# ScalarE instead of VectorE copies attention's turned probabilities, and the work ahead of the second block's output projection is put in another order

## What is computed

```python
for l in range(2):                                   # first block
    x = x + 0.5 * swiglu_ffn(rms_norm(x), ...)
    uv, c_q, c_kv, k_rope, z, xbc, dt, gates = split(rms_norm(x) @ w_in)
    merged = (g0 * (gmlp(uv) @ w_branch0)
              + g1 * (mla(c_q, c_kv, k_rope) @ w_branch1)     # causal attention, 8 heads
              + g2 * (ssd(z, xbc, dt) @ w_branch2))
    x = x + merged @ w_out
    x = x + 0.5 * swiglu_ffn(rms_norm(x), ...)
# second block
o = delta_rule(...); o = o * rsqrt(mean(o*o) + eps) * gain * silu(z)      # 512 columns
y = gelu(s5(u));     y = y * sigmoid(y @ w_glu + b_glu)                   # 512 columns
x = x + concat(o, y) @ w_out
x = x + cross_attention(rms_norm(x), mem)
return rms_norm(x + swiglu(rms_norm(x)))
```

## Time and profile before

| | us |
|---|---|
| Median of 3 runs (lowest, highest) | 1829.95 (1828.91, 1839.23) |
| The profiled execution | 1829.92 |
| Its span on the core, first to last instruction | 1828.1 |
| TensorE busy in the span | 1789.1 (98%) |
| VectorE busy | 1046.3 (57%) |
| ScalarE busy | 818.6 (45%) |
| GpSimd busy | 77.6 (4%) |

### The profile page before, as it was taken

How to read it: one execution, slowest core, us unless ns; L and a number is a source line. 1 busy time by engine, 2 the same in 40 slices (tenths; PEclk the granted TensorE clock), 3 DMA queues, 4 the chain that set the end, 5 groups by cost and what they waited for, 6 DMA issues and landing times.

```text
span 1828.1 us, 27099 instructions
## 1 busy us (share of the span) xinstructions
PE 1789.1 (98%) x11448; PEld 1584.1 (87%) x11448; DVE 1046.3 (57%) x1226; ACT 818.6 (45%) x885; POOL 77.6 (4%) x145
## 2 busy tenths in 40 slices
PE   8999999999999999999999999999999999999998
PEld 8998797877999899987978779998887976889996
DVE  4555356887655455553669876455666534545553
ACT  4554345552654445543555526544123123535542
POOL 0000000000000000000000001000561100000000
PEclk9999999999999999999999999999999999999999
DMA  7537255444655645372555446855254223436371
GB/s 253 184 125 282 81 165 160 156 148 138 207 180 192 213 151 184 120 286 81 165 164 159 141 138 208 186 196 207 92 162 79 72 90 115 139 122 213 126 276 58
DMA packets 194332, 293.15 MB, mean 160 GB/s; under 512 B 9298, under 2 KB 128884, under 8 KB 194244
## 3 DMA queue, kind: packets, MB, share of 16 engines
q1 hardware_dynamic: 191988, 287.72, 46.6%
q0 software_dynamic: 1936, 4.14, 2.1%
q10 hardware_dynamic: 320, 0.01, 0.0%
HBM read 289.49 MB, written 2.36 MB: 160 GB/s over the span
## 4 chain that ended last, share of the span: by engine, by line
PE 90%; DVE 4%; ACT 3%; DMA 2%; issue 1%; ACTq 0%; DVEq 0%; SPq 0%
PE acc L225 22%; PE acc L226 22%; PE acc L227 22%; PE acc L271 3%; PE acc L194 2%; PE acc L206 2%; PE acc L3030 2%; PE acc L462 1%; DMA ring<-in_ffn_w_in 1%; PE acc L2725 1%; PE acc L253 1%; PE acc L1304 1%; ACT big L1432 1%; ACT part_hi L216 1%; PE turn L1409 1%
## 5 line engine op out<-in xcount | busy, mean ns | idle before, releaser
L430 DVE TENSOR_TENSOR w_lo<-ring,w_hi 128x2048 fp32r<-128x2048 f32 x160 | 361.9, 2290 | 211.4 <-ACT w_hi L426 211.3
L225 PE MATMUL acc<-xT_hi,w_hi 128*128 128x256 f32 x1680 | 476.0, 283 | 1.2 <-DVE w_lo L430 0.8
L227 PE MATMUL acc<-xT_hi,w_lo 128*128 128x256 f32 x1680 | 475.4, 283 | 0.0
L226 PE MATMUL acc<-xT_lo,w_hi 128*128 128x256 f32 x1680 | 475.4, 283 | 0.0
L426 ACT ACTIVATE w_hi<-ring 128x2048 fp32r<-128x2048 f32 x160 | 301.3, 1912 | 150.1 <-PE acc L227 99.6
L225 PEld LDWEIGHTS acc<-xT_hi,w_hi 128*128 128x128 f32 x1680 | 322.5, 192 | 1.7 <-DVE w_lo L430 1.0
L226 PEld LDWEIGHTS acc<-xT_lo,w_hi 128*128 128x128 f32 x1680 | 322.5, 192 | 0.0
L227 PEld LDWEIGHTS acc<-xT_hi,w_lo 128*128 128x128 f32 x1680 | 322.5, 192 | 0.0
L225 PE MATMUL acc<-w_hi,hT_hi 128*128 128x512 f32 x440 | 172.3, 392 | 0.0
L227 PE MATMUL acc<-w_hi,hT_lo 128*128 128x512 f32 x440 | 171.3, 389 | 0.0
L226 PE MATMUL acc<-w_lo,hT_hi 128*128 128x512 f32 x440 | 171.3, 389 | 0.0
(11 more groups left out here) (550 smaller groups left out, 2978.7 us busy)
## 6 DMA issues: line engine op xcount, KB each, us to landing
ring<-in_ffn_w_in SPq DMA_DIRECT2D x88, 1024.0 KB, 6.1
ring<-in_w_in SPq DMA_DIRECT2D x52, 1024.0 KB, 5.0
ring<-in_ffn_w_out SPq DMA_DIRECT2D x44, 1024.0 KB, 6.4
ring<-in_w_branch SPq DMA_DIRECT2D x12, 1024.0 KB, 5.1
ring<-in_w_out SPq DMA_DIRECT2D x12, 1024.0 KB, 4.9
ring<-in_w_gate SPq DMA_DIRECT2D x11, 1024.0 KB, 5.2
ring<-in_w_up SPq DMA_DIRECT2D x11, 1024.0 KB, 6.8
ring<-in_w_down SPq DMA_DIRECT2D x11, 1024.0 KB, 6.0
```

Source lines behind the costliest of these rows:

```text
L225: pe.matmul(o, a_hi, wh, start=start, stop=False)
L226: pe.matmul(o, a_hi, wl, start=False, stop=False)
L227: return pe.matmul(o, a_lo, wh, start=False, stop=stop)
L430: vec.tensor_tensor(w_part(w_lo, r), raw_part(c0, r), w_part(w_hi, r).bitcast(F32), ALU.subtract).then_inc(f.lo, 1)
```

## The change

Two edits. First, in both layers the six copies of the turned probabilities become ScalarE's: `qs_vec6` turns into `qs_act4`, and stands in ScalarE's order between the high part of chunk 7 and that of chunk 8. TensorE's waits for these copies are moved from VectorE's counter to ScalarE's (the copies count 20 to 25 there), and VectorE's counter ends at 48 instead of 54. Second, in the second block `rc_vec` is cut in three (`rc_vec`, `rc_out_vec`, `rc_turned_vec`), `glu_vec` moves ahead of the norm of o, the y half is split before the o half, and on both engines the rest or high part of chunk 1 is put between them. TensorE's products of chunk 0 now wait for both halves' `late_x_lo`, since that of o comes second.

```diff
@@ qs_pt_pe, qs_vec6, qs_pv_pe @@
                 for r, (m, kb, hf) in enumerate(TURNS):
                     pe.wait_ge(qs.vec, 44 + 2 * m)
                     if r >= 4:
-                        pe.wait_ge(qs.vec, 47 + r - 4)
+                        pe.wait_ge(qs.act, 20 + r - 4)
...
-            def qs_vec6(vec):
+            def qs_act4(act):
                 for r, (m, kb, hf) in enumerate(TURNS):
-                    vec.wait_ge(qs.pe, 17 + r)
+                    act.wait_ge(qs.pe, 17 + r)
                     dst = PT1[:, kb, 4 * hf:4 * hf + 4, :] if m else PT0[:, 4 * hf:4 * hf + 4, :]
-                    vec.tensor_copy(dst, turn[r % 4][:, :].rearrange("p (h n) -> p h n", h=4)).then_inc(qs.vec, 1)
+                    act.activation(dst, turn[r % 4][:, :].rearrange("p (h n) -> p h n", h=4), ACT.Copy).then_inc(qs.act, 1)
             def qs_pv_pe(pe):
-                pe.wait_ge(qs.vec, 52)
+                pe.wait_ge(qs.act, 25)
...
-            BRANCH_IN = {0: (gm.vec, 7), 1: (qs.vec, 54), 2: (sd.vec, 31)}
+            BRANCH_IN = {0: (gm.vec, 7), 1: (qs.vec, 48), 2: (sd.vec, 31)}
@@ mixer_act @@
-                tail_part_act(act, 6, 7, 8)
+                tail_part_act(act, 6, 7)
+                qs_act4(act)
+                tail_part_act(act, 8)
                 branch_in_act(act, 2)
@@ mixer_vec @@
                 tail_part_vec(vec, 7)
                 branch_gate_vec(vec, 0, 1)
-                qs_vec6(vec)
                 tail_part_vec(vec, 8)
@@ second block @@
-        def out2_x_act(act):
-            for i, ready in enumerate(((rc.vec, RC_DONE), (gl.vec, GLU_DONE))):
-                act.wait_ge(*ready)
-                act.activation(late_x_hi[:, 4 * i:4 * i + 4, :], xT[:, 4 * i:4 * i + 4, :], ACT.Copy).then_inc(late.act, 1)
...
+        def out2_x_act(act, i):
+            act.wait_ge(*((rc.vec, RC_DONE), (gl.vec, GLU_DONE))[i])
+            act.activation(late_x_hi[:, 4 * i:4 * i + 4, :], xT[:, 4 * i:4 * i + 4, :], ACT.Copy).then_inc(late.act, 1)
+
+        def out2_x_vec(vec, i):
+            ks = slice(4 * i, 4 * i + 4)
+            vec.wait_ge(late.act, LATE_X["out2"] + 2 - i)
+            vec.tensor_tensor(late_x_lo[:, ks, :], xT[:, ks, :], late_x_hi[:, ks, :].bitcast(F32), ALU.subtract).then_inc(late.vec, 1)
@@ rc_vec @@
                     ins.then_inc(rc.vec, 1)
+
+        def rc_out_vec(vec):
             for m in range(MT):
                 vec.wait_ge(rc.act, 5 + m)
...
+        def rc_turned_vec(vec):
             for m in range(MT):
                 vec.wait_ge(rc.pe, 13 + m)
@@ second_pe @@
-            late_group_pe(pe, G_WO2, 0, (1, 2))
+            late_group_pe(pe, G_WO2, 0, (2, 2))
@@ second_act @@
-            late_act(act, 0, 1)
-            out2_x_act(act)
+            late_act(act, 0)
+            out2_x_act(act, 1)
+            late_act(act, 1)
+            out2_x_act(act, 0)
             late_act(act, 2)
@@ second_vec @@
             rc_vec(vec)
+            glu_vec(vec)
+            rc_out_vec(vec)
             late_vec(vec, 0)
-            glu_vec(vec)
+            out2_x_vec(vec, 1)
+            rc_turned_vec(vec)
             late_vec(vec, 1)
-            out2_x_vec(vec)
+            out2_x_vec(vec, 0)
             late_vec(vec, 2, 3, 4, 5)
```

## The result

| | before | changed |
|---|---|---|
| Median, us (lowest to highest, 10 runs each) | 1836.92 (1828.91 to 1843.73) | 1820.79 (1816.13 to 1828.28) |
| Ratio, 95% interval | | 0.9936 [0.9918, 0.9955] |
| The profiled execution / its span, us | 1829.92 / 1828.1 | 1821.73 / 1820.0 |

The account below looks back on a forecast made before the run. TensorE was taken to bound the kernel, 90% of the span, losing time at three stalls and the slow clock behind them. 3.80 + 3.75 + 4.99 = 12.54 us off 1829.92 gave 1817.4 us, range 1814 to 1823.

Parts of the forecast that it names:

- Which stalls, and what they cost: TensorE's waits: 4.2 us in two for attention's copies, 3.2 us in one for `late_x_lo` at the projection; all would go.
- Attention's way: TensorE from first transpose to the values' products: 12.26 and 12.21 us, to save 3.80 in layer 0, 3.75 in layer 1.
- The projection's 4.99: Second block's output projection: products end 4.99 us earlier, 3.16 of them idle time and 1.83 slow clock.
- ScalarE keeps up: At attention ScalarE is free, copies take 0.62 us each, nothing waits; they would start to cost at 0.9 us.
- Rival 3: At attention ScalarE's copies are slow, 2 us each, so the first edit gives nothing: 1824.9 us; 3%.
- The second block's order: VectorE's new order ends the last `late_x_lo` at 1529.02, 0.58 us before TensorE can use it.
- rival 2: A new small stall at the projection, 0.5 us and at worst 1.83 us of clock: about 1820 us; 10%.
- Clock: 4.8 us at the three places: Behind the three stalls the clock stays up once they are gone, 4.8 us of the predicted gain.
- one or two falls put into the range: Behind the first edit clock falls may appear or vanish; one or two, about 1.6 us each, widen the range.
- So each stall costs twice: At the three stalls TensorE loses the wait and then a slow clock: 0.43 us per product instead of 0.23.
- Rival 4: In layer 1's second feed-forward part, chunks come later, 16.8 us lost: 1834 us; 3%.
- A run of this kernel can be told from no change from about 1%: For the whole kernel, 18.3 us needed to tell a change: 1811.6 or 1848.2; within 95%, faster 3%, slower 2%.

Follow-up runs that it names:

- e7: The changed kernel with each of ScalarE's six copies cut into 8 pieces of 128x64; 0.9948 of the time of the kernel before.
- e4: The kernel before with VectorE's six copies moved ahead of the rest of chunk 7 and a gating, still on VectorE; 0.9958 of the kernel before.
- e6: The kernel before with only `glu_vec` moved ahead of the norm of o, the halves keeping their order; 0.9971 of the kernel before.
- e5: The kernel before with its three stalls filled by 128x256 products that nobody reads; 0.9979 of the kernel before.
- e1: The changed kernel run again without any edit; 0.9927 of the kernel before.
- e11: The changed kernel run a third time without any edit; 0.9933 of the kernel before.
- e3: The kernel before with only the second edit, the second block's new order; 0.9972 of the kernel before.
- e2: The kernel before with only the first edit, the copies moved to ScalarE; 0.9960 of the kernel before.

## Why the prediction was right, and where it was not

- **Which stalls, and what they cost: right.** The three waits went as named. Attention's way was to save 3.80 and 3.75 us and saved 3.96 twice: from start to start the 24 transposes took 409.01 - 406.47 = 2.54 us and not 2.87 (1.91 / 16 had a modelled end in it), and the 24 products 5.76 and not 5.59. The projection's 4.99 was 4.96. Sum 12.88 for 12.54.
- **ScalarE keeps up: right, with about the room that was counted.** The first copy starts 0.64 us after the first transpose, where I counted 0.48, but a copy takes 0.51 us in a row instead of 0.62, and by e7 it would cost from about 0.8 us on instead of 0.9. The Trainium skill's rule that VectorE is up to three times faster per element ("Trainium Architecture — The Big Picture", "The five engines, in one table") isn't borne out for this copy: 0.51 us beside VectorE's 0.61 in e4. Rival 3 stays out.
- **The second block's order: right in time, partly for a reason that wasn't needed.** The margin was 0.82 us for 0.58 predicted, so rival 2 did not come. Only the move of `glu_vec` counts (e6).
- **Clock: 4.8 us at the three places, right (e5); elsewhere, one or two falls put into the range, and that was needed.** Ahead of TensorE's last product and away from the three ways, falls cost 6.8 us in the profiled execution before and 10.2 in the changed one. These 3.4 us are most of the 4.7 that separate 8.19 from 12.88. In e1 they cost 8.5 us and in e11 3.4, so that they come out even on the mean isn't shown. e1 and e11 show that the same program draws its falls anew in each execution. That agrees with the Trainium skill ("TensorE: Matmul & The Clock Gate", Part 1), by which the monitor runs free of the program. "So each stall costs twice" is too strong: in e4 a stall of 3.17 us cost only itself.
- **Rival 4: not seen at its size.** TensorE's wait for `w_lo` is 1.3 us for 0.8, and 0.6 to 1.7 in the other runs; behind the longest, in e7, the clock fell (1166 to 1170).
- **The step that failed is the last one**, "A run of this kernel can be told from no change from about 1%", with 95% for "within". The gain lies within 1%, as forecast, but ten runs a side tell it from nothing with 0.19% to either side, so this was a clear gain and the text called it one that couldn't be told. The same step rested the base on three runs: "the same to 0.03" held for their median, 1829.95, but ten runs, spread over 15 us, gave 1836.92. (The changed kernel's ten runs show where such a spread comes from: the mean granted clock is 0.990 in the slowest, 1828.28 us, and 0.996 in the fastest, 1816.13.) So the predicted time came out 3.4 us below the measured median, while the medians lie 16.1 us apart, not 12.5. That 1820.79 lies between 1814 and 1823 is luck: counted from 1836.92, the same sum gives 1824.4, above the range. The ratio gives 11.8 us (8 to 15), which holds the 12.5.

## What to carry to other kernels

When a transpose chain stalls because its banks are copied out late, look first at what stands ahead of the copies in that engine's queue: moving one call gave the same as changing the engine. Judge such an edit by the distance between two instructions on the bounding engine, which repeats to 0.2 us where no fall of the clock lies between them, and by many runs; a single pair of profiles mixes in the clock's falls, 1.7 or 3.4 us each here, and showed 8 us of 13.

## What the runs showed of the hardware

- TensorE's clock fell to 0.50 within or behind a block of 32 products of 128x8 that kept the engine busy, in 9 of 11 executions in layer 0 and 6 of 11 in layer 1; with the same products spread between wide ones, in none of 3 executions in either layer.
- The stall of 2.1 us at the attention was followed by a fall in all six cases (before, e3 and e6, two layers each); the longer one at the projection, 3.2 us, in two of three (before and e2, not e4). With the stalls filled by products that nobody reads, e5 shows no fall at the three places.
- A ScalarE copy of 128x64 from PSUM takes 5.70 / 48 = 0.119 us in a row, so eight of them cost 0.95 us where one of 128x512 costs 0.51.
